# Cross-attention's out projection: squares ahead of the take, three feed-forward tiles split in it, the first gated rows formed in the output's rows

## The chip, the cores and the metric

The kernel runs on one core of one Trainium2 chip. The metric is the time of one execution on the device in microseconds, as the median of several runs. The core has five engines that run side by side and wait for each other through semaphores: TensorE (PE, matmuls into the eight banks of PSUM), VectorE (DVE), ScalarE (ACT), GpSimd (POOL) and SyncE (SP, which here issues the loads). Work in float32 goes through TensorE as three products: a weight and an operand are each split into a high and a low part, and hi·hi, hi·lo and lo·hi are added up.

## What is computed

Three transformer blocks in a row on one sequence of 1024 tokens and 1024 channels. The change touches the third, from the end of its mixers on:

```python
def third_block(...):
    ...
    m = jnp.concatenate([attn.astype(x.dtype), rec.astype(x.dtype)], axis=-1) @ w_out[l]
    x = x + rms_norm_3(m, mix_post_norm[l])
    h = rms_norm_3(x, ca_pre_norm[l])
    mem_n = rms_norm_3(mem, mem_norm[l])
    c = memory_cross_attention(h, mem_n, ca_wq[l], ca_wk[l], ca_wv[l], ca_wo[l])   # ends in o @ wo
    x = x + rms_norm_3(c, ca_post_norm[l])
    h = rms_norm_3(x, ffn_pre_norm[l])
    y = conv_ffn(h, ffn_w_up[l], ffn_conv_w[l], ffn_conv_b[l], ffn_w_down[l])
    x = x + rms_norm_3(y, ffn_post_norm[l])

def conv_ffn(h, w_up, conv_w, conv_b, w_down):
    u = h @ w_up                       # 1024 -> 2 * 2816 channels
    u = ...                            # causal depthwise convolution of width 3, plus conv_b
    gate, val = jnp.split(u, 2, axis=-1)
    return (jax.nn.gelu(gate, approximate=True) * val) @ w_down
```

## The kernel before, in words

Channels stand on the 128 partitions and tokens in the free dimension, so an activation is eight tiles (KT = 8) of 128 x 1024. Tokens go in two halves of 512, since a PSUM bank holds 512; `hf` is the half and `k` or `m` the channel tile. A weight tile of 1024 x 128 comes as four chunks of 128 x 256. SyncE loads the raw values, ScalarE writes a chunk's high part (`split_hi`), GpSimd its low part (`split_lo`), and TensorE runs 12 matmuls on it for one half. Slots for split chunks are a ring (eight in the out projections, five in the feed-forward), so a high part waits until TensorE has used the chunk that many places earlier. Each engine's order is the order in which the code writes its instructions; nothing is scheduled.

`memory_and_cross_attention` is one phase. Its tiles t = 0 to 15 are the mixers' out projection (two halves of eight), then keys and values of the memory, the queries, the attention, and tiles O + u, u = 0 to 15, cross-attention's out projection. Both out projections are followed by a norm, which `PostNorm` runs beside them: VectorE takes a product out of PSUM (`take`), ScalarE squares it (`square`), VectorE adds the square up (`add_square`), TensorE sums over the partitions (`total`), ScalarE makes the inverse root (`inverse_root`), VectorE scales and adds to the residual x (`renew`). For the next norm ScalarE makes the high part of x times its gain and x squared (`high`), VectorE the low part and the sum of squares (`low`, `add_next_square`). In cross-attention's out projection half 0 is so prepared; half 1 is left to the next phase. In the memory part, VectorE also scales the eight tiles of the normed memory (memT) behind take 7.

A phase ends when all engines are through (line 89). `Core.phase` (line 80) frees the semaphores of earlier phases, with a second barrier, when they and the new phase's are more than 130 together (lines 84 to 87).

`conv_ffn_and_store` is the next and last phase. It computes two up tiles of f = 0 and f = 1 (gate and value) as plain products, and all later f as a "pair", a scheme of seven products of 512 x 512 blocks in place of eight. For it VectorE forms sums of blocks of x (`form`), ScalarE their high parts (`highs`) and VectorE their low parts (`lows`, and `low` for t3). `t_made` counts the low parts. Chunks of a pair that are sums of raw blocks are formed on GpSimd (`sums_and_lo`). `drain` takes a pair's products, `conv` and `gate` and `split_gated` give the gated row, and `down` multiplies two gated rows by their part of w_down: the first down projection follows the pair of f = 2 and waits for the gated rows of f = 0 and 1 (`gated_made`). In between ScalarE applies gelu, in whose queue the later splits of the pair stand behind it.

## Time and profile before

| | us |
|---|---|
| median of 3 runs (lowest to highest) | 3349.46 (3347.65 to 3350.18) |
| span of the profiled execution | 3348.2 |
| TensorE at work in the span | 3210.3 (96%) |
| VectorE, ScalarE, GpSimd at work | 2097.9, 1224.1, 1574.1 |
| cross-attention's out projection, first to last matmul | 2494.3 to 2587.1 |
| from the feed-forward's first matmul to its first down projection | 94.5 |

A row of the timeline gives the start and the length in us, the engine, the line, the operation, the output and inputs by the program's names, and in brackets how long the engine stood idle ahead of it and which instruction ended that. Consecutive matmuls overlap, so their pace is read from their starts. TensorE's clock has two levels, 1.2 and 2.4 GHz; the granted clock is given as a share of the higher.

### The profile page before, as it was taken

To read this page: it belongs to the slowest core of one execution; us is meant where nothing else is said; L and a number is where in the kernel's file an instruction comes from. 1 tells how busy PE (TensorE), PEld (TensorE's weight loads), DVE (VectorE), ACT (ScalarE), POOL (GpSimd) and SP (SyncE) were. 2 spreads that over 40 slices of the span, in tenths; PEclk is the share of its full clock that TensorE was granted. 3 is DMA by queue.
4 is the path that set the end of the run, shared out by engine and by line. 5 is a ranking of instruction groups with operands and counts; after the bars stand their busy time and mean duration, and the time that the engine had idled before them with its cause. 6 is when DMAs were issued, how large, how long until landed. Compare 5 with 4: busy or idle time off the path is not lost. (4 is left out here: it accounts for less than half of the span.)

```text
span 3348.2 us, 42855 instructions
## 1 busy us (share of the span) xinstructions
PE 3210.3 (96%) x15940; PEld 2545.3 (76%) x15940; DVE 2097.9 (63%) x2621; ACT 1224.1 (37%) x2334; POOL 1574.1 (47%) x1662
## 2 busy tenths in 40 slices
PE   8999999999999999999899999899998899999997
PEld 6777878788888877876586688776867678788776
DVE  5544233866666677855755666655135888788887
ACT  4333133422222243334743644543144522322324
POOL 3222333666555543321043255351204577877884
PEclk9999999999999999999999999999999899999998
DMA  3011112111111111121021011043302211121113
GB/s 103 26 27 29 41 32 60 41 54 54 53 52 51 54 34 54 42 54 29 18 57 29 23 32 32 26 129 101 49 13 63 98 54 45 51 60 51 48 49 140
DMA packets 333890, 172.31 MB, mean 51 GB/s; under 512 B 78336, under 2 KB 325632, under 8 KB 333696
## 3 DMA queue, kind: packets, MB, share of 16 engines
q1 hardware_dynamic: 330352, 161.30, 17.1%
q10 hardware_dynamic: 3344, 8.39, 0.7%
q8 instruction: 125, 2.05, 0.3%
q14 instruction: 69, 0.57, 0.1%
HBM read 161.26 MB, written 8.39 MB: 51 GB/s over the span
## 5 line engine op out<-in xcount | busy, mean ns | idle before, releaser
L463 POOL TENSOR_TENSOR cf_lo<-cf_raw,cf_hi 128x256 fp32r<-128x256 f32 x317 | 318.7, 1025 | 145.1 <-ACT cf_hi L456 144.2
L240 POOL TENSOR_TENSOR ff_lo<-ff_raw,ff_hi 128x256 fp32r<-128x256 f32 x242 | 227.6, 943 | 271.2 <-ACT ff_hi L219 261.9
L333 POOL TENSOR_TENSOR om_lo<-out_raw,om_hi 128x256 fp32r<-128x256 f32 x160 | 128.4, 817 | 307.3 <-ACT om_hi L327 307.3
L456 ACT ACTIVATE cf_hi<-cf_raw 128x256 fp32r<-128x256 f32 x317 | 130.4, 417 | 355.1 <-PE psum_all L502 330.4
L264 PE MATMUL psum_all<-h_hi,ff_hi 128*128 128x512 f32 x576 | 235.4, 409 | 10.1 <-DVE h_lo L706 4.2
L463 POOL TENSOR_TENSOR ff_lo<-ffp_raw,ff_hi 128x256 fp32r<-128x256 f32 x194 | 169.7, 880 | 142.5 <-ACT ff_hi L456 142.5
L264 PE MATMUL psum_all<-h_hi,ff_lo 128*128 128x512 f32 x576 | 226.5, 393 | 0.0
L264 PE MATMUL psum_all<-h_lo,ff_hi 128*128 128x512 f32 x576 | 226.1, 393 | 0.0
L231 POOL CAST ff_hi<-ff_raw 128x256 fp32r<-128x256 f32 x116 | 54.8, 472 | 322.5 <-PE psum_all L264 307.8
L2635 DVE TENSOR_TENSOR x_resid<-x_resid,psum_all 128x1024 f32<-128x1024 f32 x112 | 136.8, 1222 | 93.3 <-PE psum_all L502 92.5
L240 POOL TENSOR_TENSOR out_lo<-out_raw,out_hi 128x256 fp32r<-128x256 f32 x120 | 116.4, 973 | 164.8 <-ACT out_hi L219 157.7
L502 PE MATMUL psum_all<-ff_hidden_hi,ff_hi 128*128 128x512 f32 x480 | 186.8, 389 | 2.7 <-DVEq L2642 2.7
L502 PE MATMUL psum_all<-ff_hidden_lo,ff_hi 128*128 128x512 f32 x480 | 186.7, 389 | 0.0
L502 PE MATMUL psum_all<-ff_hidden_hi,ff_lo 128*128 128x512 f32 x480 | 186.7, 389 | 0.0
L502 PE MATMUL psum_all<-h_hi,cf_hi 128*128 128x512 f32 x404 | 166.4, 412 | 17.8 <-POOL cf_lo L463 7.7
L456 ACT ACTIVATE ff_hi<-ffp_raw 128x256 fp32r<-128x256 f32 x194 | 80.7, 418 | 257.9 <-PE psum_all L502 251.8
L349 PE MATMUL psum_all<-h_hi,om_hi 128*128 128x512 f32 x384 | 152.8, 398 | 11.9 <-POOL om_lo L333 9.4
L502 PE MATMUL psum_all<-h_lo,cf_hi 128*128 128x512 f32 x404 | 160.9, 398 | 0.0
L502 PE MATMUL psum_all<-h_hi,cf_lo 128*128 128x512 f32 x404 | 160.6, 397 | 0.0
L264 PE MATMUL psum_all<-ff_in_hi,ff_hi 128*128 128x512 f32 x384 | 153.6, 400 | 3.3 <-issue 3.3
L264 PEld LDWEIGHTS psum_all<-h_hi,ff_hi 128*128 128x128 f32 x576 | 109.1, 189 | 55.7 <-issue 23.7
L349 PE MATMUL psum_all<-h_lo,om_hi 128*128 128x512 f32 x384 | 150.8, 393 | 0.0
(528 smaller groups left out, 9032.8 us busy)
## 6 DMA issues: line engine op xcount, KB each, us to landing
ff_raw<-w_in_dram SPq DMA_DIRECT2D x104, 256.0 KB, 2.9
cf_raw<-ffn_w_up_dram SPq DMA_DIRECT2D x88, 256.0 KB, 2.9
cf_raw<-ffn_w_down_dram SPq DMA_DIRECT2D x52, 256.0 KB, 2.7
ffp_raw<-w_up_dram SPq DMA_DIRECT2D x41, 256.0 KB, 2.7
ffp_raw<-w_down_dram SPq DMA_DIRECT2D x41, 256.0 KB, 2.7
out_raw<-w_out_dram SPq DMA_DIRECT2D x32, 256.0 KB, 2.7
out_raw<-w_in_dram SPq DMA_DIRECT2D x32, 256.0 KB, 2.8
out_raw<-ca_wo_dram SPq DMA_DIRECT2D x32, 256.0 KB, 2.7
```

The lines of the kernel that those rows point to most:

```text
L231: self.nc.gpsimd.tensor_copy(self.hi[slot][:, :], self.raw[raw][:, at:at + 2 * P]).then_inc(self.hi_ready, 1)
L240: self.nc.gpsimd.tensor_tensor(self.lo[slot][:, :], self.raw[raw][:, at:at + 2 * P], self.hi[slot][:, :].bitcast(F32), ALU.subtract).then_ ...
L264: last = self.nc.tensor.matmul(out[:, n:n + step], wt[slot][:, w], x[:, a], start=(k == 0 and m == 0), stop=(k == self.kts - 1 and m == 2))
L333: self.nc.gpsimd.tensor_tensor(self.lo[slot][:, :], self.raw[piece % self.RAWS][:, at], self.hi[slot][:, :].bitcast(F32), ALU.subtract).th ...
L349: last = self.nc.tensor.matmul(out[:, at:at + step], wt[slot][:, w], x[:, x_at], start=(k == 0 and m == 0), stop=(k == self.kts[t] - 1 and ...
L456: self.nc.scalar.activation(hi, self.source(u, c), ACT.Copy).then_inc(self.hi_ready, 1)
L463: self.nc.gpsimd.tensor_tensor(lo, self.source(u, c), hi.bitcast(F32), ALU.subtract).then_inc(self.split_done, 1)
L502: last = self.nc.tensor.matmul(out, wt[:, w], x, start=(start and k == 0 and m == 0), stop=(stop and k == 2 * len(chunks) - 1 and m == 2))
L2635: vector.tensor_tensor(row, row, core.bank(self.banks[u][m][0], T), ALU.add).then_inc(self.drained, 1)
```

## The change

- Cross-attention's out projection, and the mixers' as well: `add_square` stands ahead of the next `take`; the total of half 0 goes from behind tile 9 to ahead of the last chunk of tile 8; the inverse root and the renewing of half 0 come a tile earlier.
- In cross-attention's out projection the squares of the next norm are written into y's free rows (`high_and_square`) and are no longer added there; the adding goes to the feed-forward phase (`add_next`). Square and sum of the last tile of half 1 go there too.
- Three of the four first up tiles (12 chunks) are loaded and split in that phase (`FirstTiles`, `first_hi`, `first_lo`): a chunk behind each of the tiles 2 to 9, four at the end. This takes eight more semaphores, and one more in the feed-forward.
- The feed-forward begins with the three split tiles on half 0, then on half 1; the renewing of half 1 is on VectorE alone, no longer with GpSimd.
- The rows of f = 0 and 1 are taken into rows of y, which are free until the first down projection; the first step of their convolution is done by ScalarE (`begin`). VectorE's order is other: all forms, then lows by kind with the takes among them, then both convolutions, the drain of the first pair, and both gatings.

```diff
+    def high_and_square(self, act, hf, k):
+
+        n = (hf - self.half) * KT + k
+        act.wait_ge(self.x_new, n + 1)
+        x = self.core.x[:, self.part(hf, k)]
+        self.nc.scalar.activation(self.pair[0][:, self.part(hf, k)], x, ACT.Copy, scale=self.gain_next[:, k:k + 1]) \
+            .then_inc(self.hi_made, 1)
+        self.nc.scalar.activation(self.y[:, self.part(hf, k)] if k else self.x_acc[hf], x, ACT.Square).then_inc(self.x_squared, 1)
...
+            def first_lo(n):
+                pool.wait_ge(first_high, n + 1)
+                hi, lo = first.slots[n]
+                nc.gpsimd.tensor_tensor(lo, first.source(n), hi.bitcast(F32), ALU.subtract).then_inc(first_low, 1)
+
             for t in range(TILES):
                 st.split_lo(pool, t)
+                if O + 2 <= t < O + 10:
+                    first_lo(t - O - 2)
+            for n in range(8, 12):
+                first_lo(n)
+            pool.wait_ge(first_low, 12)
...
+                    if t == KT and chunk == KT // 2 - 1:
+                        post.total(pe, 0, 4)
                     st.product(pe, core.bank(t % 4), h, t, BANK, hf * BANK, only=(chunk,))
...
-                st.product(pe, core.bank(u % 4), h, O + u, BANK, hf * BANK)
-                if u == KT + 1:
-                    after.total(pe, 0, 4)
+                for chunk in range(KT // 2):
+                    if u == KT and chunk == KT // 2 - 1:
+                        after.total(pe, 0, 4)
+                    st.product(pe, core.bank(u % 4), h, O + u, BANK, hf * BANK, only=(chunk,))
...
+            def first_hi(n):
+                if n % 2 == 0:
+                    act.wait_ge(first_loaded[n // 2], 16)
+                if n >= 8:
+                    act.wait_ge(st.used, st.chunk0[O + 2 * KT - 2] + n - 8 + 1)
+                nc.scalar.activation(first.slots[n][0], first.source(n), ACT.Copy).then_inc(first_high, 1)
+
             for u in range(2, 2 * KT):
-                st.split_hi(act, O + u)
-                after.square(act, *divmod(u - 2, KT))
                 if u == 10:
                     after.inverse_root(act, 0, 4)
-                for k in {12: (0,), 13: (1, 2), 14: (3, 4), 15: (5,)}.get(u, ()):
-                    after.high(act, 0, k)
+                st.split_hi(act, O + u)
+                if u < 10:
+                    first_hi(u - 2)
+                after.square(act, *divmod(u - 2, KT))
+                for k in {10: (0,), 11: (1,), 12: (2,), 13: (3,), 14: (4, 5), 15: (6,)}.get(u, ()):
+                    after.high_and_square(act, 0, k)
+            for n in range(8, 12):
+                first_hi(n)
             after.square(act, 1, KT - 2)
-            after.high(act, 0, KT - 2)
-            after.square(act, 1, KT - 1)
-            after.high(act, 0, KT - 1)
+            after.high_and_square(act, 0, KT - 1)
+            act.wait_ge(after.x_squared, KT)
...
+                if t and (t - 1) % KT:
+                    post.add_square(dve, *divmod(t - 1, KT))
                 st.wait_product(dve, t)
                 post.take(dve, hf, m, core.bank(t % 4))
...
-                if t and (t - 1) % KT:
-                    post.add_square(dve, *divmod(t - 1, KT))
+                if t >= 8:
+                    post.renew(dve, own, 0, t - 8)
                 if t >= 9:
-                    post.renew(dve, own, 0, t - 9)
-                if t >= 10:
-                    next_low(0, t - 10)
+                    next_low(0, t - 9)
...
             for u in range(2 * KT):
+                if u and (u - 1) % KT:
+                    after.add_square(dve, *divmod(u - 1, KT))
+                if u == 2 * KT - 1:
+                    after.low(dve, 0, KT - 1)
                 st.wait_product(dve, O + u)
                 after.take(dve, *divmod(u, KT), core.bank(u % 4))
-                if u and (u - 1) % KT:
-                    after.add_square(dve, *divmod(u - 1, KT))
-                for k in {10: (0,), 11: (1,), 12: (2, 3), 13: (4,), 14: (5, 6), 15: (7,)}.get(u, ()):
+                for k in {8: (0,), 9: (1,), 10: (2,), 11: (3,), 12: (4, 5), 13: (6,), 14: (7,)}.get(u, ()):
                     after.renew(dve, own, 0, k)
-                for k in {12: (0,), 13: (1, 2), 14: (3, 4), 15: (5,)}.get(u, ()):
+                for k in {9: (0,), 10: (1,), 11: (2,), 12: (3,), 13: (4, 5), 14: (6,)}.get(u, ()):
                     after.low(dve, 0, k)
-                    after.add_next_square(dve, 0, k)
-            after.add_square(dve, 1, KT - 1)
-            for k in (KT - 2, KT - 1):
-                after.low(dve, 0, k)
-                after.add_next_square(dve, 0, k)
-
-
-def conv_ffn_and_store(core, a, y, post, last, taps, bias, out):
+            dve.wait_ge(after.y_taken, 2 * KT)
...
-            post.total(pe, 1, 4, here=False)
-            for hf in range(2):
-                for t in range(2):
-                    st.product(pe, [(core.bank(2 * t + hf), half(h, hf))], range(4 * t, 4 * t + 4),
-                               ready=post.next_made if (hf, t) == (1, 0) else None, release=hf == 1)
-            post.next_total(pe, 6)
-            st.product(pe, whole(4, h), range(8, 12))
+            for t in range(3):
+                st.product(pe, [(core.bank(2 * t), half(h, 0))], range(4 * t, 4 * t + 4), release=False)
+                if t == 0:
+                    pe.wait_ge(post.y_summed, 1)
+                    post.total(pe, 1, 7, here=False)
+            for t in range(3):
+                st.product(pe, [(core.bank(2 * t + 1), half(h, 1))], range(4 * t, 4 * t + 4),
+                           ready=post.next_made if t == 0 else None)
+                if t == 1:
+                    pe.wait_ge(post.x_summed, 2 * (KT - 1))
+                    post.next_total(pe, 6, here=False)
             pe.wait_ge(rstd_ready, 1)
             st.product(pe, whole(6, h), range(12, 16))
...
+            nc.scalar.activation(post.sq[(KT - 1) % 2], y[:, post.part(1, KT - 1)], ACT.Square).then_inc(post.y_squared, 1)
             nc.scalar.preload_act_table_set(EXP_LN)
-            post.inverse_root(act, 1, 4)
-            split(0)
-            split(1)
+            post.inverse_root(act, 1, 7)
             for k in range(KT):
-                post.high(act, 1, k)
+                post.high_and_square(act, 1, k)
                 if k >= 4:
                     for n in (k - 4, k):
                         act.dma_start(out[n * P:(n + 1) * P, :], x[:, n * T:(n + 1) * T]).then_inc(spilled[k - 4], 16)
             scale(0)
-            split(2)
             scale(1)
-            highs(0)
+            split(3, 0, 1)
             scale(2)
-            highs(1)
             scale(3)
             post.next_inverse_root(act, 6, rstd_ready)
-            split(3)
+            split(3, 1)
             nc.scalar.preload_act_table_set("gelu_and_others")
-            highs(2)
-            highs(3)
+            for k in range(4):
+                highs(k)
...
                 split(u, 0, 2)
                 if f % 2 and f < LAST:
                     gelu(f - 1)
-                elif f == 2:
-                    gelu(0)
                 split(u, 2, 5)
                 if f == 2:
+                    begin(0)
                     act.wait_ge(st.used, 16)
...
-                split(u, 7, 11)
+                if f == 2:
+                    split(u, 7, 9)
+                    begin(1)
+                    split(u, 9, 11)
+                    gelu(0)
+                else:
+                    split(u, 7, 11)
                 if f % 2 == 0 or f == LAST:
                     gelu(f - 1)
                 split(u, 11)
...
+            def finish_conv(f):
+                for s in range(2):
+                    src, to = opening[f][s], opening[f][2 + s]
+                    dve.wait_ge(begun, 2 * f + s + 1)
+                    for step, back in ((0, 2), (1, 1)):
+                        own.link(vector.scalar_tensor_tensor(out=to[:, back:], in0=src[:, 0:T - back], scalar=tap(f, s, step),
+                                                             in1=to[:, back:], op0=ALU.mult, op1=ALU.add))
+                    if s == 0:
+                        dve.sem_inc(conv_made, 1)
+
+            def gate_opening(f):
+                dve.wait_ge(gelu_made, f + 1)
+                row = opening[f][2]
+                own.link(vector.tensor_tensor(row, opening[f][3], row, ALU.mult))
+                hi, lo = gated_row(f)
+                own.link(vector.tensor_copy(hi, row))
+                own.link(vector.tensor_tensor(lo, row, hi.bitcast(F32), ALU.subtract))
+                dve.sem_inc(gated_made, 1)
...
+            dve.wait_ge(post.y_squared, 1)
+            vector.tensor_tensor(post.acc[1], post.acc[1], post.sq[(KT - 1) % 2], ALU.add).then_inc(post.y_summed, 1)
+            for k in range(1, KT):
+                add_next(0, k, k - 1)
             for k in range(KT):
-                post.scale_for_pool(dve, 1, k)
-                if k >= 2:
-                    post.low(dve, 1, k - 2)
-                    post.add_next_square(dve, 1, k - 2)
-            for k in (KT - 2, KT - 1):
-                post.low(dve, 1, k)
-                post.add_next_square(dve, 1, k)
-            form(0)
-            form(1)
+                post.renew(dve, own, 1, k)
+                if k >= 1:
+                    post.low(dve, 1, k - 1)
+            post.low(dve, 1, KT - 1)
+            dve.wait_ge(post.x_squared, KT)
+            for k in range(1, KT):
+                add_next(1, k, KT - 2 + k)
+            dve.wait_ge(st.used, 4)
+            for k in range(4):
+                form(k)
             lows(0)
-            form(2)
-            lows(1)
-            form(3)
-            lows(2)
-            lows(3)
             dve.wait_ge(rstd_ready, 1)
             take_tiles(0)
-            for step in range(3):
-                conv(0, 0, row2, step)
-            for step in range(3):
-                conv(0, 1, row0, step)
-            gate(0)
-            split_gated(0)
+            lows(1)
+            take_tiles(1)
             for k in range(4):
                 low(*t3(k), t3_held(k), 12 + k + 1)
-            take_tiles(1)
-            for step in range(3):
-                conv(1, 0, row2, step)
-            for step in range(3):
-                conv(1, 1, row0, step)
-            gate(1)
-            split_gated(1)
+            lows(2)
+            finish_conv(0)
+            finish_conv(1)
             drain(2)
+            gate_opening(0)
+            gate_opening(1)```

What the order of the instructions becomes is shown at three places. First VectorE in the mixers' out projection, from take 6 on. `COPY mix` is a take, `work<-work` the adding of a square, `memT` the memory's scaling. Before:

```order
L828 COPY mix_15090<-psum_all 128x512
L3570 SCALAR_TENSOR_TENSOR memT<-memT,g_mem_norm,work 128x256 x8
L841 TENSOR_TENSOR work<-work 128x512
L828 COPY mix_15090<-psum_all 128x512
L841 TENSOR_TENSOR work<-work 128x512
```

and now:

```order
L849 TENSOR_TENSOR work<-work 128x512
L836 COPY mix_15090<-psum_all 128x512
L3619 SCALAR_TENSOR_TENSOR memT<-memT,g_mem_norm,work 128x256 x8
L849 TENSOR_TENSOR work<-work 128x512
L836 COPY mix_15090<-psum_all 128x512
```

The square of tile 7 is added right behind the memT scalings in both, but it is now ahead of take 8, and TensorE's total waits for it in tile 8. Second, the phase's end on VectorE, from the last take on, and GpSimd at the boundary. Before:

```order
L828 COPY mix_15090<-psum_all 128x512
L841 TENSOR_TENSOR work<-work 128x512
L862 SCALAR_TENSOR_TENSOR mix_15090<-mix_15090,g_ca_post_norm,work 128x512
L869 TENSOR_TENSOR x_resid<-x_resid,mix_15090 128x512
L897 SCALAR_TENSOR_TENSOR h_lo<-x_resid,g_ffn_pre_norm,h_hi 128x512
L908 TENSOR_TENSOR work<-work,rstd 128x512
L841 TENSOR_TENSOR work<-work 128x512
```

and now, VectorE and then GpSimd:

```order
L914 SCALAR_TENSOR_TENSOR h_lo<-x_resid,g_ffn_pre_norm,h_hi 128x512
L836 COPY mix_15090<-psum_all 128x512
L89 UNCONDITIONAL_BRANCH
L4024 UNCONDITIONAL_BRANCH
L4146 TENSOR_TENSOR work<-work 128x512
```

```order
L3359 TENSOR_TENSOR first_lo<-first_raw,first_hi 128x256 x4
L89 UNCONDITIONAL_BRANCH
L85 ISA
L3823 UNCONDITIONAL_BRANCH
```

Behind the last take stood 11 more steps (the first seven are shown); now none does. Between the phases GpSimd has an instruction of line 85, the freeing of semaphores, that was not at this boundary before. Third, ScalarE in the pair of f = 2; `L3942` is gelu, `L464` a high part, `L3948` the convolution's first step:

```order
L3988 ACTIVATE work<-psum_all 128x512
L464 ACTIVATE first_hi<-cf_sum 128x256
L464 ACTIVATE first_hi<-cf_raw_23746 128x256
L3948 ACTIVATE mix_15090<-mix_15090,g_ffn_bias,g_ffn_taps 128x1024 x2
L464 ACTIVATE first_hi<-cf_raw_23746 128x256
L464 ACTIVATE first_hi<-cf_raw_23744 128x256
L3942 ACT_TABLE_LOAD
L3942 ACTIVATE mix_15090<-mix_15090 128x1024 x2
L464 ACTIVATE cf_hi_23742<-cf_raw_23744 128x256
```

and VectorE behind the pair's first low parts:

```order
L4059 SCALAR_TENSOR_TENSOR mix_15090<-mix_15090,g_ffn_taps 128x1023
L4078 TENSOR_TENSOR cf_both<-work,psum_all 128x512
L4080 TENSOR_TENSOR work<-cf_both,psum_all 128x512
L4083 TENSOR_TENSOR work<-work,psum_all 128x512
L4085 TENSOR_TENSOR work<-cf_both,psum_all 128x512
L4086 TENSOR_TENSOR work<-work,psum_all 128x512
L4090 TENSOR_TENSOR work<-work,psum_all 128x512
L4099 TENSOR_TENSOR work<-work,psum_all 128x512
L4067 TENSOR_TENSOR mix_15090<-mix_15090 128x1024
L4069 CAST gated_hi<-mix_15090 128x1024
L4070 TENSOR_TENSOR gated_lo<-mix_15090,gated_hi 128x1024
```

Before, the first gelu stood behind the pair's second chunk and the second ahead of the last three, and both rows were gated ahead of the drain (`L4078` to `L4099`). Now both gelus stand ahead of the last three chunks, and the gatings behind the drain.

## Rows read from the trace of the kernel before

**Rows 1.** Busy time by stretch, feed-forward's opening: stretch, length, engines, granted clock, DMA.

```profile
2596.25:2690.75 94.50, 77.12 (x282) 57.16 (x283) 81.47 (x80) 48.58 (x85) 56.59 (x46) 0.87 0.27 92
```

**Rows 2.** TensorE's waits, 2494 to 2700: waiting line, engine waited for, total, times, longest.

```profile
PE psum_all L502 <- POOL cf_lo L463: 8.7, 4, 3.1
PE psum_all L502 <- DVE h_lo L897: 5.5, 4, 2.1
```

**Rows 3.** Timeline of TensorE, its last out projection tile to the first down projection.

```profile
2581.37 0.47 PE L349 MATMUL psum_all<-h_hi,om_hi 128*128 128x512 f32 x1 [2.38 <-POOL om_lo L333]
...
2596.25 2.05 PE L847 MATMUL psum_all<-work,ones 128*128 128x512 f32 x2 [9.19 <-PEq L89]
...
2690.75 0.47 PE L502 MATMUL psum_all<-gated_hi,cf_hi 128*128 128x512 f32 x1 [2.26 <-issue]
...
2692.26 0.63 PE L502 MATMUL psum_all<-gated_hi,cf_hi 128*128 128x512 f32 x1
...
2695.25 0.54 PE L502 MATMUL psum_all<-gated_lo,cf_hi 128*128 128x512 f32 x1
```

**Rows 4.** Timeline, mixers' out projection and keys: VectorE, ScalarE, then TensorE.

```profile
2228.32 5.14 DVE L3570 SCALAR_TENSOR_TENSOR memT<-memT,g_mem_norm,work 128x256 f32<-128x256 f32 x8
...
2231.86 0.42 ACT L327 ACTIVATE om_hi<-out_raw 128x256 fp32r<-128x256 f32 x1 [1.00 <-PE psum_all L349]
...
2271.95 7.07 PE L3348 MATMUL psum_all<-memT,kv_raw 128*128 128x256 f32 x32
...
2282.49 22.67 PE L3348 MATMUL psum_all<-memT,kv_raw 128*128 128x256 f32 x96 [2.62 <-DVE ca_kT L3548]
```

**Rows 5.** The boundary ahead of the mixers' out projection: VectorE's last, ScalarE's first, the clear.

```profile
2176.53 0.69 DVE L3225 TENSOR_TENSOR mix<-work,wh_decay 128x512 f32<-128x512 f32 x1
...
2178.59 1.33 ACT L327 ACTIVATE om_hi<-out_raw 128x256 fp32r<-128x256 f32 x4 [4.10 <-PEq L86]
...
L85 POOLq EVENT_SEMAPHORE_RANGE_CLEAR  x2: 392/600/807, 1651.3 to 2177.9; - x2
```

**Rows 6.** Timeline of VectorE: its steps with GpSimd idle and beside it.

```profile
2295.19 0.74 DVE L862 SCALAR_TENSOR_TENSOR mix<-mix,g_mix_post_norm,work 128x512 f32<-128x512 f32 x1
...
2296.57 0.74 DVE L897 SCALAR_TENSOR_TENSOR h_lo<-x_resid,g_ca_pre_norm,h_hi 128x512 fp32r<-128x512 f32 x1
2297.23 0.68 DVE L908 TENSOR_TENSOR work<-work,rstd 128x512 f32<-128x512 f32 x1
...
2640.87 1.28 DVE L3951 TENSOR_TENSOR x_pair<-x_resid,x_pair 128x512 fp32r<-128x512 f32 x2
...
2653.71 1.78 DVE L3951 TENSOR_TENSOR t_lo<-t_held,t_hi 128x512 fp32r<-128x512 f32 x1
2655.41 2.34 DVE L3960 TENSOR_TENSOR work<-psum_all,rstd 128x1024 f32<-128x1024 f32 x2
...
2658.64 2.60 DVE L4005 SCALAR_TENSOR_TENSOR work<-work,g_ffn_taps 128x1022 f32<-128x1022 f32 x2
...
2670.37 4.45 DVE L3951 TENSOR_TENSOR h_lo<-t_held,h_hi 128x512 fp32r<-128x512 f32 x4
...
2711.46 1.22 DVE L4013 TENSOR_TENSOR work<-work 128x1024 f32<-128x1024 f32 x1
...
2715.60 0.70 DVE L4017 CAST gated_hi<-work 128x1024 fp32r<-128x1024 f32 x1
```

**Rows 7.** Timeline of ScalarE: a round of highs, a scale, inverse root's second half; GpSimd.

```profile
2633.32 1.16 ACT L3851 ACTIVATE x_pair<-x_resid 128x512 fp32r<-128x512 f32 x2 [0.89 <-DVE t_held L3946]
2634.39 0.62 ACT L3851 ACTIVATE t_hi<-t_held 128x512 fp32r<-128x512 f32 x1
2634.91 2.18 ACT L3846 ACTIVATE x_resid<-x_resid,g_ffn_pre_norm 128x1024 f32<-128x1024 f32 x2
...
2641.76 1.06 ACT L924 ACTIVATE rstd<-rstd 128x1024 f32<-128x1024 f32 x1
...
2682.10 9.57 POOL L463 TENSOR_TENSOR cf_lo<-cf_raw,cf_hi 128x256 fp32r<-128x256 f32 x8 [6.01 <-ACT cf_hi L456]
```

135 lines of the change are left out of this document (94 added, 41 removed).

## Prediction

> **What bounds the kernel now.** By the page's busy times TensorE is at work for 96% of the span (the table above). It has the same matmuls before and after, so time can only come from stretches in which it stands still or runs at the lower of its two clocks. I therefore read, in this order: the table of stretches, to find where its busy share falls; the waits of TensorE there; its timeline, for the size and the place of each gap; and the timelines of the engines that end the gaps. The table shows the weak stretch: in the 94.5 us from the start of the feed-forward phase to its first down projection TensorE is busy for 77.1 at a mean granted clock of 0.87 [rows 1]. The waits name 8.7 us in four waits for GpSimd's splits and 5.5 in four for half 1's low parts [rows 2]. The timeline puts the longest of all, 9.19 us at the phase boundary, ahead of 2596.25, so the out projection's last matmul ends at E = 2587.06, and the first down projection's matmul starts at 2690.75 [rows 3]. From E to there is 103.7 us. After it a run of eight matmuls starts 0.43 apart, where full clock gives 0.23; that is 1.5 us more, 105.2 in all.
>
> **1. The mixers' out projection (t = 0 to 15).** Two things change. Squares are added ahead of the take, and the total of half 0 goes from behind tile 9 into tile 8, ahead of its last chunk. On VectorE the eight scalings of memT stand between take 7 and the last square: they run 5.14 us from 2228.32 [rows 4], so the square is added at 2233.4 and done at 2234.0. ScalarE's split at 2231.86, which TensorE's third chunk of tile 8 releases, shows TensorE ready for the last chunk at 2231.8 [rows 4]. Before, nothing stood there; now the total waits: a **new stall of 2.2 us**. It may cost clock too. Gaps of such a size show both: after 2.38 no matmul is slow, after 2.26 eight are [rows 3], so 0 to 1.6, and I take 0.8. Against this VectorE ends its work on half 0 earlier: renew 7 and low 6 no longer stand behind tile 15's square, and TensorE's wait of 2.62 for the first key copy [rows 4] goes. Some 3.5 us of VectorE work (renew 1.38, two pairs of low and add at 1.26, one of them partly under a wait) moves ahead of that copy, which need be only 2.6 earlier. With it goes the slow clock behind the wait: 96 matmuls took 22.67, and at the pace of the 32 before (0.221) they take 21.2, so 1.5. Sum: +3.0 − 4.1 = **−1.1**.
>
> **2. Cross-attention's out projection.** ScalarE's queue gets a first split (0.42) per tile, GpSimd's a first lo (eight took 9.57 beside a busy VectorE, 1.2 each [rows 7]). Per tile of 5.44 us GpSimd then has five of them, 6.0 at that price and less where VectorE rests, and eight slots give two tiles of slack; I cost them at nothing, and at up to 2 us if that cover fails. Here no memT work stands before the square: it is added some 3.1 us behind tile 7, and the total comes 4.1 behind it, so no stall. What goes is the wait of 2.38 at 2581.37 [rows 3]: ScalarE there stood behind VectorE's sums of the next squares, which this phase no longer makes. **−2.4**.
>
> **3. The boundary.** VectorE's last work now is take 15, at E + 0.9, instead of 8.9 behind E. But eight new semaphores push the phase past the limit of 130, and the order shows it: GpSimd gets a clear of the semaphores with a second barrier between the phases. The trace has such a boundary: VectorE ends at 2177.2, the clear runs, and ScalarE starts at 2178.59, 1.4 later [rows 5]; the plain one took 0.3. So TensorE starts at S = E + 2.4, where it started at E + 9.2.
>
> **4. From S to the first down projection.** TensorE starts at once, since three tiles are split. Its order is no longer the bound; VectorE's and ScalarE's are, and I follow those. Tile 0, half 0: 24 × 0.227 = 5.4; total 1.0; inverse root 1.4: VectorE begins to renew half 1 at **S + 7.9**. Renewing takes 1.38 and a low 0.66, from the starts of three rows [rows 6]; eight rounds end with the last low at S + 24.9. GpSimd has no work here, so the fast rows hold. TensorE, which reaches half 1 at S + 17, waits some 3 us on the last lows, which is not on the path. Then ScalarE: four scales at 2.1 (8.4, S + 33.8; the last may wait for its spill), one split 0.4, the inverse root 2.1 (twice the 1.06 of its second half), three splits 0.9, a table load 1.3, and four rounds of highs at 1.59 [rows 7] give S + 45. VectorE's seven sums (0.7 each) and four forms (2.7 each) end at S + 41 and are covered by it. From **S + 45** VectorE has: the four tile takes at 2.34 a pair, 4.7; four lows each of t2, t3 and t4 at 1.1 [rows 6], 13.2; and eight convolution steps at 1.30, 10.4: S + 73.3, and with small waits **S + 74**. ScalarE's second gelu stands ahead of the last three splits of the pair, and it needs six of the eight steps: it ends at S + 72.6. So the chunk that TensorE wants at about S + 65 is ready at S + 74.3: **the stall is back, 9 us of it**. The 18 matmuls left then run slow at first (13 at 0.43 and 5 at 0.23): S + 81.3. VectorE's last drain step ends at S + 82, and only then come the two gatings, 1.22 + 0.70 + 1.22 fast [rows 6], with GpSimd beside the first for a part 3.4 each: **S + 88.9**. TensorE waits for these 7.6 us and starts the down projection at the lower clock, which costs 13 × 0.2 = 2.8. In all 2.4 + 88.9 + 2.8 = 94.1 against 105.2, so −11.1. A fall of the clock at the boundary's gap of 2.4 adds 0 to 1.6 to tile 0 and so to the path; with 0.8 of it: **−10.3**.
>
> VectorE's prices depend on GpSimd: a step of 128 x 512 with both operands in SBUF takes 0.64 alone, 1.1 on average and 1.78 at worst beside it [rows 6]. The Trainium skill, "SBUF — State Buffer", section "Who interferes with whom", says that a tensor_tensor with both inputs in SBUF contends with GpSimd's reads, and that the loser is fully blocked. By that rule the steps could cost the worst row wherever GpSimd is busy, which is the slower rival below (3358 instead of 3335.7).
>
> **5. Behind the down projection** the order is the same on every engine, and VectorE enters it 3 us better placed, as drain 2 is done before. I cost it at nothing, ± 2.
>
> **Sum:** −1.1 − 2.4 − 10.3 = **−13.8 us**. The profiled span is 3348.2, 1.3 below the median of the runs, 3349.46; I take the difference as unchanged: 3349.5 − 13.8 = **3335.7**.
>
> **Rivals.**
> - *The stall comes back whole.* If the lows cost 1.4 instead of 1.1 and conv steps and gatings rise in proportion, by 1.27, the path is 3.6 + 2.8 + 1.8 = 8.2 us longer, and −5.6 is left: 3344. For it: low parts of half 1 already hold TensorE four times before, for 5.5 us [rows 2], beside GpSimd's additions. Against it: it needs GpSimd busy all along, and it is idle from S + 63 to S + 74 on my path.
> - *Slower than before.* VectorE's steps with both operands in SBUF are blocked each time that GpSimd works: 12 lows at 1.78 (+8.2), eight conv steps at 1.3 × 1.78 / 1.1 = 2.1 (+6.4), gatings (+3), and the last two forms, whose eight steps fall beside GpSimd's splits (+9, 4 of it covered by ScalarE). 8.2 + 6.4 + 3 + 5 = 22.6, less 13.8, is +9: 3358. With the rest in proportion it decides from a mean low of about 1.5. The four t3 lows of before took 4.45 beside GpSimd, which speaks against it.
> - *More is gained.* No clock falls at the two 2.2 to 2.4 gaps (−1.6), the second gelu and gatings come sooner, since ScalarE's highs and VectorE's lows overlap better than I let them (S + 42 instead of 45), and TensorE keeps its clock at the down projection (−2.8): −21, 3328.
> - *The change does not do what it says:* were the first splits late for the phase, TensorE would stand at S. They are released by tile 14's chunks and done 2 us before E; I give it nothing of its own.
>
> **How the numbers follow.** Forecast 0.57 (3331 to 3341), the stall whole 0.18 (3341 to 3348), more gained 0.16 (3325 to 3331), slower 0.05, something unseen 0.04. The range of 8 in 10 reaches into both neighbours, the more so as the terms that I held at one value (clock 0 to 1.6 at two places, 2 us of cover in the out projection, 2 us behind) add up to some ± 4: 3328 to 3346. A measurement of this kernel tells 0.2% (6.7 us) from no change, so faster means below 3342.8: 0.57, 0.16 and a third of the 0.18, with part of the unseen, 0.80; within, 0.15; slower 0.05.
>
> **What would show it.** In the trace of after: (1) a wait of TensorE of about 2 us at the total in tile 8, and none before the third key; (2) no wait at the out projection's last tile; (3) the boundary at 2.4, with a clear on GpSimd; (4) VectorE's first renew 8 us behind TensorE's start, its first t1 low at 40 to 45; (5) a wait of some 9 us for a GpSimd split in the first pair, behind ScalarE's second gelu, and one of 7 to 8 for the gated rows, each with eight or more slow matmuls. I am wrong if (5) is missing (then more is gained), or if VectorE's lows show 1.5 us and more (then less).

## The result, and the profile after

The changed kernel takes 3330.47 us (median of four runs, 3329.85 to 3331.45) against 3349.43 for the kernel before beside it: ratio 0.9948, 95% interval 0.9937 to 0.996, or 19.0 us. Forecast were 3335.7, so 13.8 less, in a range of 3328 to 3346. The profiled spans are 3329.7 and 3348.2 us. The kernel before was run many more times beside the experiments: its 51 executions go from 3342.97 to 3350.51 us with a median of 3348.11, and against that the gain is 17.6. One execution of a variant below (e8) took 3987.6 us at a granted clock of 0.76 and is left out of its median.

The table cuts the run at eight places that both traces show: A, the first matmul of the mixers' out projection; O, the first of cross-attention's; E, the end of its last; S, the feed-forward's first; D, the first down projection's; T, the first matmul that needs the last two gated rows of half 0, behind a pause for them; U, the total of half 0 behind that; Z, the last transposes.

| stretch | before | after | difference | forecast |
|---|---|---|---|---|
| start to A | 2179.87 | 2180.08 | +0.2 | 0 |
| A to O (mixers, memory, attention) | 314.43 | 311.09 | −3.3 | −1.1 |
| O to E (out projection) | 92.76 | 89.66 | −3.1 | −2.4 |
| E to S (boundary) | 9.19 | 2.56 | −6.6 | −6.8 |
| S to D | 94.50 | 90.66 | −3.8 | −4.8 |
| D to T | 592.65 | 593.17 | +0.5 | +1.3 |
| T to U | 19.99 | 17.58 | −2.4 | 0 |
| U to Z | 38.77 | 38.78 | 0 | 0 |
| sum | 3342.16 | 3323.58 | −18.6 | −13.8 |

(The forecast's −10.3 for E to D is here its 91.3 us and 0.8 of clock ahead of D, and 1.3 of clock behind it; of its −11.6 ahead of D the row of the boundary holds 6.8.)

TensorE's waits of after from 2491 to 2680 us (columns as in [rows 2]) answer to the 8.7 and 5.5 us there:

```profile
PE psum_all L510 <- POOL cf_lo L471: 9.8, 1, 9.8
PE psum_all L510 <- DVEq L4071: 7.9, 1, 7.9
PE psum_all L510 <- PEq L86: 2.6, 1, 2.6
PE psum_all L349 <- DVE h_lo L3648: 2.4, 1, 2.4
PE psum_all L510 <- DVE h_lo L914: 2.0, 2, 1.1
```

The table of stretches, S to D, answers to [rows 1]: TensorE busy for 71.01 us of 90.66 at a mean granted clock of 0.90, and VectorE for 81.21, nine tenths of the stretch.

```profile
2583.39:2674.05 90.66, 71.01 (x282) 55.35 (x283) 81.21 (x96) 49.55 (x78) 28.02 (x27) 0.90 0.24 85
```

TensorE's timeline of after, at the total in tile 8, at the boundary and at the two long waits, answers to [rows 3]. The 2.38 us ahead of the last out projection tile are gone; the two long waits came as forecast, 9.77 and 7.85.

```profile
2232.84 0.67 PE L855 MATMUL psum_all<-work,ones 128*128 128x512 f32 x1 [1.00 <-DVE work L849]
...
2583.39 0.76 PE L510 MATMUL psum_all<-h_hi,first_gated_hi 128*128 128x512 f32 x1 [2.56 <-PEq L86]
2583.95 0.63 PE L510 MATMUL psum_all<-h_lo,first_gated_hi 128*128 128x512 f32 x1
...
2659.16 0.80 PE L510 MATMUL psum_all<-h_hi,cf_hi 128*128 128x512 f32 x1 [9.77 <-POOL cf_lo L471]
...
2674.05 0.80 PE L510 MATMUL psum_all<-gated_hi,first_hi 128*128 128x512 f32 x1 [7.85 <-DVEq L4071]
```

VectorE's timeline of after, from its forms' end to the gatings. From the start of renewing at 2592.77 to 2662 it waits for nothing; its one wait ahead of the gatings is the 3.42 ahead of the drain's last step (L4099).

```profile
2624.87 1.78 DVE L4034 TENSOR_TENSOR x_resid<-x_resid 128x512 f32<-128x512 f32 x1
2626.68 1.67 DVE L4036 TENSOR_TENSOR x_resid<-x_resid 128x512 f32<-128x512 f32 x1
2628.39 0.69 DVE L4038 TENSOR_TENSOR t_held<-x_resid 128x512 f32<-128x512 f32 x1
2629.00 2.49 DVE L4043 TENSOR_TENSOR x_pair<-x_resid,x_pair 128x512 fp32r<-128x512 f32 x4
2631.41 2.35 DVE L4052 TENSOR_TENSOR mix<-psum_all,rstd 128x1024 f32<-128x1024 f32 x2
2633.68 5.04 DVE L4043 TENSOR_TENSOR x_pair<-x_resid,x_pair 128x512 fp32r<-128x512 f32 x4
...
2640.90 4.03 DVE L4043 TENSOR_TENSOR h_lo<-t_held,h_hi 128x512 fp32r<-128x512 f32 x4
2644.85 3.02 DVE L4043 TENSOR_TENSOR t_lo<-t_held,t_hi 128x512 fp32r<-128x512 f32 x4
2647.80 10.72 DVE L4059 SCALAR_TENSOR_TENSOR mix<-mix,g_ffn_taps 128x1022 f32<-128x1022 f32 x8
...
2666.24 0.69 DVE L4099 TENSOR_TENSOR work<-work,psum_all 128x512 f32<-128x512 f32 x1 [3.42 <-PE psum_all L510]
2666.84 1.75 DVE L4067 TENSOR_TENSOR mix<-mix 128x1024 f32<-128x1024 f32 x1
```

### The profile page after: what moved, and what is told of

Its sections match the earlier page's. It is cut to its first block and busy times, and to the rows that moved or that the text cites. A ratio compares the mean times of both kernels' runs of the same rounds, so it can differ in the third digit from the quotient of the medians.

```text
span 3329.7 us, 42857 instructions
## 1 busy us (share of the span) xinstructions
PE 3199.8 (96%) x15940; PEld 2539.3 (76%) x15940; DVE 2090.8 (63%) x2625; ACT 1228.5 (37%) x2338; POOL 1552.6 (47%) x1654
## 3 DMA queue, kind: packets, MB, share of 16 engines
q8 instruction: 125, 2.05, 0.2%
## 5 line engine op out<-in xcount | busy, mean ns | idle before, releaser
L471 POOL TENSOR_TENSOR first_lo<-cf_raw,first_hi 128x256 fp32r<-128x256 f32 x247 | 242.7, 996 | 106.8 <-ACT first_hi L464 105.8
L333 POOL TENSOR_TENSOR om_lo<-out_raw,om_hi 128x256 fp32r<-128x256 f32 x160 | 130.5, 830 | 290.6 <-ACT om_hi L327 289.6
L471 POOL TENSOR_TENSOR ff_lo<-ffp_raw,ff_hi 128x256 fp32r<-128x256 f32 x194 | 169.5, 879 | 143.0 <-ACT ff_hi L464 142.9
L464 ACT ACTIVATE first_hi<-cf_raw 128x256 fp32r<-128x256 f32 x247 | 101.8, 417 | 288.8 <-PE psum_all L510 262.7
L2653 DVE TENSOR_TENSOR x_resid<-x_resid,psum_all 128x1024 f32<-128x1024 f32 x112 | 136.8, 1221 | 93.5 <-PE psum_all L510 92.8
L510 PE MATMUL psum_all<-ff_hidden_hi,ff_hi 128*128 128x512 f32 x480 | 186.8, 389 | 2.7 <-DVEq L2660 2.7
L510 PE MATMUL psum_all<-ff_hidden_lo,ff_hi 128*128 128x512 f32 x480 | 186.7, 389 | 0.0
L510 PE MATMUL psum_all<-ff_hidden_hi,ff_lo 128*128 128x512 f32 x480 | 186.7, 389 | 0.0
L464 ACT ACTIVATE ff_hi<-ffp_raw 128x256 fp32r<-128x256 f32 x194 | 80.7, 418 | 257.9 <-PE psum_all L510 251.8
L349 PE MATMUL psum_all<-h_hi,om_hi 128*128 128x512 f32 x384 | 152.6, 397 | 10.1 <-POOL om_lo L333 7.7
L349 PE MATMUL psum_all<-h_lo,om_hi 128*128 128x512 f32 x384 | 150.6, 392 | 0.0
L349 PE MATMUL psum_all<-h_hi,om_lo 128*128 128x512 f32 x384 | 150.4, 392 | 0.0
L264 PE MATMUL psum_all<-ff_in_hi,ff_lo 128*128 128x512 f32 x384 | 150.1, 391 | 0.0
L264 PE MATMUL psum_all<-ff_in_lo,ff_hi 128*128 128x512 f32 x384 | 150.0, 391 | 0.0
```

What stands on the lines that cost most here:

```text
L264: last = self.nc.tensor.matmul(out[:, n:n + step], wt[slot][:, w], x[:, a], start=(k == 0 and m == 0), stop=(k == self.kts - 1 and m == 2))
L333: self.nc.gpsimd.tensor_tensor(self.lo[slot][:, :], self.raw[piece % self.RAWS][:, at], self.hi[slot][:, :].bitcast(F32), ALU.subtract).th ...
L349: last = self.nc.tensor.matmul(out[:, at:at + step], wt[slot][:, w], x[:, x_at], start=(k == 0 and m == 0), stop=(k == self.kts[t] - 1 and ...
L464: self.nc.scalar.activation(hi, self.source(u, c), ACT.Copy).then_inc(self.hi_ready, 1)
L471: self.nc.gpsimd.tensor_tensor(lo, self.source(u, c), hi.bitcast(F32), ALU.subtract).then_inc(self.split_done, 1)
L510: last = self.nc.tensor.matmul(out, wt[:, w], x, start=(start and k == 0 and m == 0), stop=(stop and k == 2 * len(chunks) - 1 and m == 2))
```

## The experiments

All but the last start from the changed kernel. The theory: two parts of the change stand each for itself (A to O, O to E), and behind E one queue, VectorE's, sets the time of D. The rival to that: TensorE's wait of 9.8 us lies on the path in full, and taking it away would gain 9.8. In the table E–S and S–D are the boundary and the stretch to the first down projection.

| kernel | median us | ratio to before (95%) | A–O | O–E | E–S | S–D |
|---|---|---|---|---|---|---|
| before | 3349.43 | 1 | 314.4 | 92.8 | 9.2 | 94.5 |
| changed | 3330.47 | 0.9948 (0.9937 to 0.996) | 311.1 | 89.7 | 2.56 | 90.7 |
| e1 mixers as before | 3335.03 | 0.9961 (0.9947 to 0.9975) | 314.6 | 89.8 | 2.57 | 90.8 |
| e4 sums back | 3333.52 | 0.9953 (0.9937 to 0.997) | 311.2 | 89.7 | 5.25 | 91.2 |
| e2 no clear | 3328.87 | 0.9941 (0.9924 to 0.9958) | 311.3 | 89.6 | 1.67 | 89.3 |
| e6 two tiles | 3329.28 | 0.9944 (0.9927 to 0.9961) | 312.1 | 89.8 | 2.16 | 89.8 |
| e3 splits ahead | 3328.01 | 0.9939 (0.9922 to 0.9955) | 312.2 | 89.8 | 2.57 | 88.2 |
| e7 gatings in the drain | 3326.02 | 0.9934 (0.9917 to 0.995) | 311.2 | 89.7 | 2.56 | 85.6 |
| e5 both | 3327.08 | 0.9936 (0.992 to 0.9953) | 311.2 | 89.7 | 2.57 | 86.1 |
| e9 total early | 3326.98 | 0.9939 (0.9924 to 0.9955) | 312.4 | 89.8 | 2.57 | 88.1 |
| e8 e7, sums on GpSimd | 3330.61 | 0.995 (0.993 to 0.997) | 311.1 | 89.7 | 2.57 | 93.1 |
| e10 e7 + e2 + e9 | 3322.26 | 0.9926 (0.9912 to 0.994) | 312.3 | 89.9 | 1.67 | 82.4 |
| e11 e10, casts on ScalarE | 3316.84 | 0.9908 (0.9893 to 0.9923) | 311.3 | 89.7 | 1.67 | 79.5 |

Each ratio is against the kernel before as run beside that version, where its median was 3347.8 to 3349.4. The intervals overlap from one version to the next, so single edits are judged by their stretch; a second profile of the kernel before (last experiment) repeats its four within 0.02 us. But a stretch carries clock too. In S to D there is one such place: behind its wait of 9.8 us TensorE runs the pair's last 18 matmuls, 6 to 14 of them slow in kernels that do the same there, and where the gatings stand behind the drain, its last step waits for them. From TensorE's resumption to that step it is 7.1 us in the changed kernel and in e1, 7.2 and 7.3 in e4 and e9, but 6.1 in e2 and 6.0 in e6. For these the end of VectorE's convolution, ahead of that place, is given as well; in the changed kernel it is S + 75.1.

**e1: the mixers' out projection as before.**

```diff
-                    if t == KT and chunk == KT // 2 - 1:
-                        post.total(pe, 0, 4)
...
+                if t == KT + 1:
+                    post.total(pe, 0, 4)
...
-                if t and (t - 1) % KT:
-                    post.add_square(dve, *divmod(t - 1, KT))
                 st.wait_product(dve, t)
...
-                if t >= 8:
-                    post.renew(dve, own, 0, t - 8)
+                if t and (t - 1) % KT:
+                    post.add_square(dve, *divmod(t - 1, KT))
                 if t >= 9:
-                    next_low(0, t - 9)
+                    post.renew(dve, own, 0, t - 9)
```

> The changed kernel with the mixers' out projection alone put back as before: squares behind the take, total of half 0 behind tile 9, inverse root and renewing a tile later. Theory (this part is a term of its own, worth what the trace shows between the first matmul of the phase and the first of cross-attention's out projection, 311.1 us against 314.4 before): that stretch goes back to 314.4 (the 2.6 us wait ahead of the third key and a slow stretch behind it return, the 1.0 us wait at the total goes), and the span is 3.3 us longer than the changed kernel's, about 3333 us. Rival (the stretch shrank by chance of the clock alone, since the total's new wait costs what the key's wait cost): within 1 us of the changed kernel.

A to O is 314.6 again, +3.5, the other three stretches stay within 0.2, and TensorE's wait for the first key copy is back:

```profile
2282.47 1.07 PE L3385 MATMUL psum_all<-memT,kv_raw 128*128 128x256 f32 x2 [2.64 <-DVE ca_kT L3596]
```

This part is a term of its own, and it is worth three times what was forecast.

**e4: the next norm's sums back in the out projection.** Only their place moves; the squares keep their own rows.

```diff
                 if u == 2 * KT - 1:
                     after.low(dve, 0, KT - 1)
+                    next_sum(KT - 1)
...
                     after.low(dve, 0, k)
+                    next_sum(k)
...
-            for k in range(1, KT):
-                add_next(0, k, k - 1)
```

> The changed kernel with the seven sums of half 0's next squares put back into cross-attention's out projection on VectorE, one behind each low part (they read y's rows, as now); the feed-forward phase no longer makes them. Theory A (before, the 2.4 us wait at the last tile came from ScalarE waiting for these sums, since squares had two buffers; with rows of their own it doesn't wait): no wait at the last tile, the out projection stays at 89.7 us, and the start of the feed-forward loses nothing, since VectorE waits 3.1 us there anyway; within 1 us of the changed kernel, the boundary up to 0.7 later. Rival B (the wait came from VectorE's time for the sums): the wait of about 2.4 us is back, +2 to +3, 3332 to 3333.

Neither came out whole. O to E stays at 89.7 with no wait at the last tile, so it isn't VectorE's time for the sums that made it (A). The wait of before had come from ScalarE, whose square stood behind a sum while squares had two buffers; ScalarE's timeline of before:

```profile
2578.23 0.63 ACT L891 ACTIVATE rstd<-x_resid 128x512 f32<-128x512 f32 x1 [4.11 <-DVE work L908]
```

With rows of their own squares don't wait for sums. e4 keeps the earlier total and renewing as well, and that these alone wouldn't have ended the wait isn't shown. But the boundary grows from 2.56 to 5.25, where A gave it 0.7. VectorE's and TensorE's timelines of e4:

```profile
2583.45 0.68 DVE L836 COPY mix<-psum_all 128x512 f32<-128x512 f32 x1
...
2585.57 0.77 PE L510 MATMUL psum_all<-h_hi,first_gated_hi 128*128 128x512 f32 x1 [5.25 <-PEq L86]
```

The last take starts 3.1 us behind the end of TensorE's last matmul (0.4 in the changed kernel), since VectorE is late by its sums. So moving the sums is not what ended the wait in the out projection, but it shortens the boundary by 2.7.

**e2: no clear at the last boundary**, by a limit of 134 instead of 130.

> The changed kernel with the limit on semaphores at 134 instead of 130, so that the last boundary (76 + 57 = 133) has no clear and no second barrier; all other boundaries stay. Theory (the clear is what the eight semaphores of the split tiles cost): from the out projection's last matmul to the feed-forward's first 1.5 us instead of 2.56, the take's end plus 0.3 to 0.4, so -1.1 us; if the shorter pause also spares the seven slow matmuls behind it, -2.5. Rival (the boundary is set by something else, a load or ScalarE's last work): no change.

```profile
2581.96 0.47 PE L510 MATMUL psum_all<-h_hi,first_gated_hi 128*128 128x512 f32 x1 [1.67 <-PEq L89]
2582.27 0.39 PE L510 MATMUL psum_all<-h_lo,first_gated_hi 128*128 128x512 f32 x1
```

E to S is 0.9 shorter, and the granted clock stays up at S (the second matmul starts 0.31 behind the first, where the changed kernel's takes 0.56 and the next five 0.43): VectorE renews at S + 8.0 instead of S + 9.4. Of these 1.4 us only 0.3 are left at the end of the convolution (S + 74.8), for the low parts take 16.6 us in all instead of 15.5, more of them beside GpSimd's splits. E to D falls from 93.2 to 91.0, but 1.0 of these 2.2 us is that TensorE ran 8 slow matmuls instead of 13 behind its wait of 9.8, which the edit doesn't touch. What the clear cost up to the end of the convolution is 1.2 us: 0.9 at the boundary and 0.3 behind it.

**e6: two tiles split ahead instead of three.**

```diff
-    st = PairStream(core, sb, [kind for kind, _, _ in tiles], first.early, made=3, place=(raws, first.ring + [fifth]))
+    st = PairStream(core, sb, [kind for kind, _, _ in tiles], first.early, made=2, place=(raws, first.ring + [fifth]))
...
             nc.scalar.preload_act_table_set(EXP_LN)
+            split(2)
             post.inverse_root(act, 1, 7)
```

> The changed kernel with two up tiles split ahead instead of three; the third's four chunks are loaded and split at the start of the feed-forward phase, ahead of ScalarE's inverse root. Theory A (only VectorE's queue counts from there on, and TensorE needs these chunks at 11 us): the down projection starts 90.7 behind TensorE's start as before, within 1 us. Rival B (each tile split ahead is worth its own; GpSimd's four low parts slow VectorE's first sums, or the load comes late and holds ScalarE's inverse root): renewing begins 1 to 4 us later, and so does the down projection: 3332 to 3335.

S to D is 89.8 and E to S 2.16: without the third tile D comes 1.3 us earlier, but 1.1 of that are the 7 slow matmuls instead of 13 behind the wait of 9.8. At the end of the convolution (S + 75.4) e6 is 0.2 ahead of the changed kernel, counted from E. So the third tile's splitting ahead brings nothing.

**e3, e7, e5: is TensorE's 9.8 us wait on the path?** e3 puts ScalarE's last three splits ahead of the gelus, which ends the wait. e7 leaves it and moves both gatings on VectorE. e5 does both.

```diff
 e3 and e5, ScalarE
-                    split(u, 9, 11)
+                    split(u, 9)
                     gelu(0)
...
 e7 and e5, VectorE
                 vector.tensor_tensor(cross, both, bank(1), ALU.add).then_inc(drained, 1)
+                if between:
+                    between()
...
-            drain(2)
-            gate_opening(0)
-            gate_opening(1)
+            drain(2, lambda: (gate_opening(0), gate_opening(1)))
```

> The changed kernel, with ScalarE's last three splits of the first pair ahead of the two gelus, so that TensorE's 9.8 us wait for the pair's chunk goes. Theory A (VectorE's queue sets the start of the first down projection): its convolution steps end where they did, 75.2 us behind TensorE's start; then drain 4.2 and gatings 7.2, no wait of 3.4 in the drain: the down projection starts 86.6 behind TensorE's start instead of 90.7, so -4 us, 3326. Rival B (TensorE's wait is on the path in full): -9.8, 3321. Rival C (the wait is hidden as a whole): no change, 3330.

> The changed kernel with one thing moved on VectorE: both opening gatings stand behind the second step of the first drain, ahead of its other four; ScalarE's order and TensorE's 9.8 us wait stay. Theory A (VectorE's queue, and in it the drain's last step, sets the down projection's start): convolution ends at 75.2 behind TensorE's start, two drain steps 1.4, gatings 7.2 to 8.5 (GpSimd splits beside the first): the down projection starts at 84 to 85.5 instead of 90.7, and TensorE, which works until 83, hardly pauses and keeps its clock: -6 to -9 us, 3322 to 3325. Rival B (the wait of TensorE for the chunk is what costs): less than 2 us gained.

> Both moves together: the last splits ahead of the gelus, and the gatings behind the drain's second step. Theory A: VectorE's convolution ends 75.2 behind TensorE's start, drain steps 1.4, gatings 7.2: the down projection starts at 83.8, -6.9 us less what 13 us of one idle stretch cost in clock (0 to 3): 3324 to 3327, no better than the gatings' move alone or a little worse, since the wait that the splits' move takes away was beside VectorE's work. Rival B (both waits are on the path): the gains add up, -10 or more, below 3321.

TensorE's timeline of e3, then VectorE's of e7:

```profile
2671.17 0.79 PE L510 MATMUL psum_all<-gated_hi,first_hi 128*128 128x512 f32 x1 [17.82 <-DVEq L4072]
```

```profile
2657.59 0.69 DVE L4080 TENSOR_TENSOR work<-cf_both,psum_all 128x512 f32<-128x512 f32 x1
2658.20 1.68 DVE L4067 TENSOR_TENSOR mix<-mix 128x1024 f32<-128x1024 f32 x1
2659.92 1.11 DVE L4069 CAST gated_hi<-mix 128x1024 fp32r<-128x1024 f32 x1
2661.06 1.63 DVE L4070 TENSOR_TENSOR gated_lo<-mix,gated_hi 128x1024 fp32r<-128x1024 f32 x1
```

In e3 the wait of 9.8 is gone and one of 17.8 stands ahead of D instead of 7.9: of 9.8 us taken away, 2.5 are gained. They are 3.8 us in VectorE's drain (its wait of 3.4 and a short one) and 0.5 at a gating that GpSimd no longer slows, less 1.9 by which the convolution ends later (S + 77.0 instead of 75.1); 1.6 of that the earlier splits cost (t4's low parts take 4.66 instead of 3.02). In e7 the wait stays at 9.8 and 5.0 are gained, by the order of VectorE's queue alone; D to T gives 1.2 of it back (594.4 instead of 593.2), in part by 14 slow matmuls at D instead of 10. e5, with both, is no better than e7 (86.1 against 85.6). So the theory of VectorE's queue holds up to the end of the convolution, and in e7 up to D; in the changed kernel TensorE's 18 matmuls are a leg of the path between the two. The sizes hold not quite: the gatings in e7 take 9.1 us and not 7.2 to 8.5, each step slowed by GpSimd's splits, and TensorE still pauses for 2.74 and resumes at the lower clock.

**e9: the total behind the first chunk.** VectorE's other wait in the stretch was 3.1 us for the inverse root. A chunk is six matmuls for one half (twelve are both halves), so the total comes 18 matmuls, some 4.1 us, earlier.

```diff
+            st.product(pe, [(core.bank(0), half(h, 0))], range(1), release=False, stop=False)
+            pe.wait_ge(post.y_summed, 1)
+            post.total(pe, 1, 7, here=False)
+            st.product(pe, [(core.bank(0), lambda k: half(h, 0)(k + 2))], range(1, 4), release=False, start=False)
```

> The changed kernel with one thing moved on TensorE: the total of half 1's squares stands behind the first chunk of the first up tile instead of behind its fourth. Theory (VectorE's queue from TensorE's start on sets the down projection's start, and its only wait there is the 3.1 us for the inverse root): the root is there at about 5.1 us, VectorE goes from its sums, which end at 6.3, straight to renewing (now at 9.4), and everything up to the down projection comes 3.1 us earlier: it starts at 87.6 behind TensorE's start instead of 90.7, about 3327.4. Rival (something else on the way, ScalarE's highs at S + 40.2 or the loads, is as late as VectorE): less than 1.5 us.

```profile
2584.27 5.04 DVE L4144 TENSOR_TENSOR work<-work,mix 128x512 f32<-128x512 f32 x7
2589.23 0.74 DVE L870 SCALAR_TENSOR_TENSOR mix<-mix,g_ca_post_norm,work 128x512 f32<-128x512 f32 x1
```

Renewing begins at S + 6.2, straight behind the sums, 3.2 us earlier than in the changed kernel, and S to D is 88.1: −2.6. At the end of the convolution (S + 72.4) 2.8 are left, since t3's low parts take 4.41 instead of 4.03 beside GpSimd; 0.2 more go in the drain's wait for TensorE. Nothing else takes over as the bound there.

**e8: the sums of half 1 on GpSimd**, on top of e7; VectorE's seven go.

```diff
+            for k in range(1, KT):
+                pool.wait_ge(post.x_squared, k + 1)
+                pool.wait_ge(post.x_summed, KT - 2 + k)
+                nc.gpsimd.tensor_tensor(post.x_acc[1], post.x_acc[1], y[:, post.part(1, k)], ALU.add) \
+                    .then_inc(post.x_summed, 1)
```

> The version with the gatings in the drain, and in it the seven sums of half 1's next squares on GpSimd, which is idle in the first 30 us of the phase, instead of VectorE (5.0 us of its queue between renewing and forms). Theory A (what bounds from renewing to the first low part, S + 26 to S + 45.6, is VectorE: sums 5.0 and forms 14.6, not ScalarE as the prediction had it): the first low part of t1 comes at S + 41 to 42, where ScalarE's highs become the bound (they started at S + 40.2), so -4 us against the version with the gatings' move (its down projection at S + 85.6 goes to about 82), less what GpSimd's additions slow VectorE's renewing (0 to 3). Rival B (ScalarE's queue is the bound there, as the prediction had it): 0 to -1. Rival C (contention eats it): renewing, 16.6 us now, takes 20 and more, and the version is no faster or slower.

Rival C. VectorE's timeline, then GpSimd's:

```profile
2595.11 0.69 DVE L877 TENSOR_TENSOR x_resid<-x_resid,mix 128x512 f32<-128x512 f32 x1
2595.72 1.78 DVE L914 SCALAR_TENSOR_TENSOR h_lo<-x_resid,g_ffn_pre_norm,h_hi 128x512 fp32r<-128x512 f32 x1
2597.43 1.78 DVE L870 SCALAR_TENSOR_TENSOR mix<-mix,g_ca_post_norm,work 128x512 f32<-128x512 f32 x1
```

```profile
2595.11 1.85 POOL L3828 TENSOR_TENSOR work<-work,mix 128x512 f32<-128x512 f32 x1 [18.10 <-ACT mix L908]
2597.16 1.49 POOL L3828 TENSOR_TENSOR work<-work,mix 128x512 f32<-128x512 f32 x1 [0.20 <-ACT mix L908]
...
2613.57 1.33 POOL L3828 TENSOR_TENSOR work<-work,mix 128x512 f32<-128x512 f32 x1 [2.63 <-ACT mix L908]
```

Six of VectorE's steps take 1.75 to 1.78 where they take 0.74 alone, 6.2 us in all for 5.0 taken off its queue, and renewing takes 22.8 us instead of 16.6. TensorE waits four times for half 1's low parts, 6.9 us in all, so the next norm's total behind them and ScalarE's inverse root are late too: the first t1 low part comes at S + 49.4, and D 7.5 later than in e7; the version takes 4.6 us more than e7. GpSimd loses little: 1.33 alone, 1.45 to 1.85 beside VectorE. The Trainium skill, "SBUF — State Buffer", section "Who interferes with whom", says that a VectorE instruction with two SBUF inputs contends with a GpSimd instruction that reads SBUF; these rows agree for six steps, with 1.0 us each. Three further steps (L877) start together with an addition and take 0.69 as alone; there it is the addition that takes longer, 1.81 to 1.85.

**e10 and e11: together.** e10 is e7, e2 and e9 at once. e11 also gives the two casts to ScalarE, ahead of its splits for the down projection; VectorE then makes both products first and both low parts behind them.

```diff
 e11, ScalarE
                 split(u, 11)
+                for n in range(2):
+                    act.wait_ge(begun, 4 + n + 1)
+                    nc.scalar.activation(gated_row(n)[0], opening[n][2], ACT.Copy).then_inc(t_high, 1)
...
 e11, VectorE
-                own.link(vector.tensor_copy(hi, row))
+                dve.wait_ge(t_high, 16 + f + 1)
```

> Three edits together on the changed kernel: gatings behind the drain's second step, limit 134 (no clear at the last boundary), total behind the first chunk. Theory (all three lie on one path, VectorE's queue, and so add up): against the 93.2 us from the out projection's last matmul to the down projection: -5.0 (gatings), -2.2 (no clear, with the clock it spares), -3.1 (total; without the clear and its slow matmuls nearer -2): 83 to 84, and a time of 3320 to 3322. Rival (TensorE's own 9.8 us wait and its work behind it take over as the bound once VectorE's queue is 8 us shorter): the down projection no earlier than 85.5, 3323 and more.

> The version of the three edits, and the two casts of the gated rows' high parts (1.1 us each beside GpSimd's splits) given from VectorE to ScalarE, which is idle there once its splits are through. Theory A (VectorE's queue is still the bound): two casts of 1.1 go and two hops of some 0.3 come, -1 to -2 us against the three edits. Rival B (ScalarE's last splits wait for TensorE's chunks, and the casts stand behind them in its queue, so the gated rows wait for TensorE): the down projection starts 2 to 4 us later than with the three edits, +2 to +4. By the trace of the gatings' version ScalarE's last split ran at S + 83, while the second gating began at S + 81.2: B is the likelier if the splits stay ahead of the casts.

e10: E to D is 84.1 against 93.2, −9.1 for 5.0, 2.2 and 2.6 apart (9.8). They add up better at the marks of the path: 0.9 at the boundary, 3.2 at the end of the convolution (S + 72.0) and 5.0 by the gatings' place are 9.1. The clock that e2 spared at S brings nothing here, since VectorE no longer waits for tile 0's end, and its 1.0 behind the wait of 9.8 is off the path once the gatings don't wait for the drain.

e11: VectorE's and GpSimd's timelines, then TensorE's at D:

```profile
2655.84 2.82 DVE L4074 TENSOR_TENSOR mix<-mix 128x1024 f32<-128x1024 f32 x2
2658.65 2.60 DVE L4079 TENSOR_TENSOR gated_lo<-mix,gated_hi 128x1024 fp32r<-128x1024 f32 x2
```

```profile
2655.02 1.42 POOL L471 TENSOR_TENSOR first_lo<-cf_raw,first_hi 128x256 fp32r<-128x256 f32 x2
2660.14 2.38 POOL L471 TENSOR_TENSOR first_lo<-cf_raw,first_hi 128x256 fp32r<-128x256 f32 x2 [3.70 <-ACT first_hi L464]
```

```profile
2661.98 0.47 PE L510 MATMUL psum_all<-gated_hi,first_hi 128*128 128x512 f32 x1 [1.08 <-POOL first_lo L471]
2662.28 0.40 PE L510 MATMUL psum_all<-gated_lo,first_hi 128*128 128x512 f32 x1
```

Expected were −1 to −2 or, by the rival, a loss; it is −3.0 in S to D and −5.4 in the median, of which 1.1 may be A to O's two values (last section) and not the edit. Since the casts stand ahead of the down projection's splits in ScalarE's queue, GpSimd has nothing to split from 2656.4 to 2660.1, and VectorE's steps run at 1.3 to 1.4 instead of 1.5 to 1.7. The gatings end 3.6 us earlier, TensorE pauses for 1.08 instead of 3.51 and keeps its clock, which makes D to T another 1.7 shorter. The rival had the casts wait behind those splits, which the edit's order excludes. e11 beats both kernels: 3316.8 us, 0.9908 of before.

**The kernel before once more.** Open were the 2.4 us from T to U.

> The kernel before, unchanged, once more, for a second profile of it. Open is the last 2.4 us of the difference between the two traces: behind the wait for the last gated rows but one, the kernel before ran 13 matmuls at the lower clock (from that wait to the total of half 0 20.0 us, against 17.6 in the changed kernel), after a wait of 2.8 us, while the changed one had none after 3.2. If the change causes it, the second profile of before shows 13 slow matmuls and 20.0 again; if it is chance of the clock, the stretch takes anything from 17.6 to 20.0, as the changed kernel's variants show it (17.6 to 18.8). Elsewhere: 103.7 us from the out projection's last matmul to the first down projection, 92.8 for the out projection, within 0.5.

```profile
3282.84 0.80 PE L502 MATMUL psum_all<-h_hi,cf_hi 128*128 128x512 f32 x1 [3.10 <-DVEq L4020]
3283.43 0.63 PE L502 MATMUL psum_all<-h_lo,cf_hi 128*128 128x512 f32 x1
```

The second profile of before runs 13 slow matmuls there again, 19.9 us. The changed kernel's resumes at full clock after 3.16 us:

```profile
3267.22 0.50 PE L510 MATMUL psum_all<-h_hi,first_hi 128*128 128x512 f32 x1 [3.16 <-DVEq L4130]
3267.56 0.40 PE L510 MATMUL psum_all<-h_lo,first_hi 128*128 128x512 f32 x1
```

Of the twelve profiles of the changed kernel and its variants ten show no slow matmuls behind this pause and two (e2, e9) seven, 1.2 us. The 13 come in 2 of 2 profiles against 0 of 12, so the kernel has a part in it. By what isn't settled; the length of the pause (2.8 and 3.1 with 13, 3.2 and 3.3 with seven, 2.8 to 3.2 with none) isn't it. Nor is it shown that every execution of the kernel before has them: both profiles are of long ones (spans of 3348.2 and 3347.6 us). The ten executions of this run have a median of 3345.38 and thirteen of the same kernel beside them 3349.49, 4.1 us apart with no edit at all; what the short ones, down to 3342.97, do differently no profile shows.

## Why the prediction was right, and where its sizes were not

**The direction and the mechanism were right.** Of the five marks that it named four came: the wait at the total in tile 8 (1.0 instead of about 2) and none before the third key, no wait at the last out projection tile, the boundary with the third clear, and the two waits of 9.77 and 7.85 (forecast 9 and 7 to 8), with 13 and 10 slow matmuls. The fourth came a little late: the first renewing at S + 9.4 (forecast 8) and the first t1 low part at S + 45.6 (40 to 45). Of the 4.8 us by which it fell short, 2.2 are in part 1, 0.7 in part 2 and 2.4 in part 5, less 0.3 in the parts between and 0.2 at the start.

**Part 1, the term that was mis-sized: −1.1 forecast, −3.3 measured, −3.5 by e1.** The new stall was put at 2.2 with 0.8 of clock; it is 1.00 without. The step that failed is the 5.14 us for the scalings of memT, taken from [rows 4]. In after they take 3.68:

```profile
2228.41 3.68 DVE L3619 SCALAR_TENSOR_TENSOR memT<-memT,g_mem_norm,work 128x256 f32<-128x256 f32 x8
2232.02 0.68 DVE L849 TENSOR_TENSOR work<-work 128x512 f32<-128x512 f32 x1
```

and the reason is on GpSimd:

```profile
2228.30 0.74 POOL L333 TENSOR_TENSOR om_lo<-out_raw,om_hi 128x256 fp32r<-128x256 f32 x1 [0.56 <-ACT om_hi L327]
2235.72 3.73 POOL L333 TENSOR_TENSOR om_lo<-out_raw,om_hi 128x256 fp32r<-128x256 f32 x4 [6.67 <-ACT om_hi L327]
```

ScalarE's inverse root now stands ahead of tile 10's splits and waits for the total, so GpSimd gets no work for 6.7 us, and VectorE, which the total waits for, runs alone. A wait that the change adds quiets the engine that would have made it longer; a duration measured beside GpSimd was carried to a place where it rests. The clock behind the key's wait gave 1.9 instead of 1.5 (22.67 against 20.98 for 96 matmuls, and the row ahead).

**Part 2: −2.4 forecast, −3.1 measured.** The wait of 2.38 went for the reason given; the rest is three slow matmuls fewer. That ScalarE's and GpSimd's extra work is hidden held: O to E is TensorE's bare time (busy 89.66 of 89.66).

**Part 3: 2.4 forecast, 2.56.** The clear was there, at 2582.6. e2 adds what the trace didn't show: without it the clock stays up at S.

**Part 4: S to D 88.9 forecast, 90.66; at the renewing 1.4 of it is clock at S** (by e2), for which the forecast had 0.8 outside its 88.9. Renewing began at S + 9.4 (7.9). Then two errors met. ScalarE's queue was said to end the wait for the first t1 low part, at S + 45. Its first highs came at S + 40.2 and weren't the bound; VectorE's forms were, 14.6 us where 10.8 were reckoned, since five of the last six steps ran beside GpSimd and took 1.1 to 1.8 each. From there 12 low parts took 12.1 instead of 13.2, t1's own four, which I had left out, 2.4, and the convolution 10.7: S + 75.1 against 74. (Behind D the forecast had 13 × 0.2 as 2.8, which is 2.6; 10 were slow there, and D to T is +0.5 instead of +1.3.) That the steps would mean about 1.0 and not 1.4 decided against the rival of the whole stall, and e8 shows what the slower-than-before rival would have needed: GpSimd beside every step, at 1.0 us each.

**What the wait of 9.8 us costs was left open.** The forecast's path came: the second gelu, the split, the 18 matmuls (S + 75.8 to 82.8; forecast 74.3 to 81.3), the drain's last step, the gatings. It called this the old stall come back, 9 us of it. But most of it passes beside VectorE's own work, and VectorE stands idle for it only 3.8 us: e3 shows that it was worth 2.5 us of 9.8, and e7 that the place of the gatings behind the drain was the dearer fault.

**Part 5: 0 ± 2 forecast, −2.4 measured**, all of it between T and U. "VectorE enters it 3 us better placed" is not what brought it: the pause ahead of T is as long as before, and the 2.4 are clock.

**Size of the range.** 3330.5 lies 0.5 below the forecast's own 3331 to 3341 (0.57) and inside "more is gained" (3325 to 3331, 0.16), for other reasons than that rival gave: no clock was kept at the boundary or at D, and the first low parts came at S + 45.6 and not 42; of its terms only the clock in tile 8 came. Of the 4.8 us that are missing, the 2.4 between T and U are clock that nothing in the forecast foresaw. Without them the time would have been some 3332.9 by this count; that it came out on this side is luck.

## What to carry to other kernels

Follow the queue of the engine that is never idle, not the longest wait of the one that is: a wait of TensorE of 9.8 us beside VectorE's 81 busy of 91 us was worth a quarter of its length, and reordering VectorE without touching it was worth twice that. Price a step of VectorE by whether GpSimd will be working at its new place, and ask whether the change itself starts or stops GpSimd's work there: this took 1.5 us off one stall, made moved sums cost more than they saved (e8), and gave e11 more than its two casts. Where edits lie on one path their gains add up, and the stretch between two marks tells them apart when whole times can't. Set the marks on the path itself and ahead of any place where the clock may fall: at D alone e2 and e6 looked 1.0 and 1.1 us better than they were.

## What the runs showed of the hardware that was not expected

- A GpSimd addition of 128 x 512 makes a VectorE step with two operands in SBUF take 1.78 us instead of 0.74, six times alike (1.75 to 1.78), and is itself slowed by 0.1 to 0.2 then (1.45 to 1.49 against 1.33) or by 0.5 when a step starts together with it, which isn't slowed at all (0.69, three times) (e8).
- A cast of 128 x 1024, with one operand, is slowed beside GpSimd too: 0.69 alone, 1.10 or 1.11 beside its splits, four times alike (e7, e10), but also 1.20 to 1.21 further on in the feed-forward in every profile, and 1.65 once in each profile of the kernel before. So no single price holds for it.
- At the last boundary a pause of 1.67 us left the clock up, three times of three (e2, e10, e11); one of 2.16 to 2.57 brought six to eight slow matmuls, seven times of seven where the total wasn't moved, at once or 0.8 us behind the resumption. Yet at T pauses of about 3 us left it up in ten profiles, took it down for seven matmuls in two, and for 13 in both of the kernel before. Behind the wait of 9.8 us, in kernels that do the same there, it is 6 to 14. Behind such a pause the cost could be bounded from rows (0 to 1.6, and here 2.6), not foretold.
- A to O comes in two values in kernels that do the same there: 311.1 to 311.3, and 312.1 to 312.4 (e3, e6, e9, e10), five slow matmuls more at its start. Medians of single edits carry this 1.1 us; their stretch S to D doesn't carry this one.
